# The last four modulation chunks of a hybrid mLSTM layer: row sums on VectorE, or partial sums on VectorE and a column reduction on TensorE

## The chip, the cores and the metric

The kernel runs on one core of a Trainium2 chip. The metric is the device time of one execution in microseconds (us). The median over three executions of the kernel before is 1634.9 us (1633.83 to 1635.89).

## The reference

One layer of a diffusion backbone is computed for 128 context tokens and 512 latent tokens (640 together, `NT`), with a model width of 1024. The part that matters here is the modulation. Two conditioning vectors (`c_ctx` for context, `c` for latent) pass through silu and a 1024 x 6144 matrix, and the 6144 results are cut into six chunks that scale and shift the activations:

```
mod_ctx = silu(c_ctx) @ w_mod[l] + b_mod[l]
mod_lat = silu(c) @ w_mod[l] + b_mod[l]
sh1, sc1, g1, sh2, sc2, g2 = jnp.split(mod, 6, axis=-1)
h = x * (1 + sc1) + sh1
out, finals = mixer(h, l, p, init, fourier_fn)
x = layer_norm(ALPHA * x + g1 * out, ...)
h2 = x * (1 + sc2) + sh2
a, u = jnp.split(h2 @ p['w_ffn_in'][l], 2, axis=-1)
f = (jax.nn.silu(a) * u) @ p['w_ffn_out'][l]
x = layer_norm(ALPHA * x + g2 * f, ...)
```

The mixer projects `h`, runs a bidirectional mLSTM over four heads and a Fourier branch, gates both, and multiplies by the output matrix.

## The kernel before

Activations are kept transposed: 128 channels on the partitions, 640 tokens along the free axis. Weights arrive in units of 128 x 1024 floats (512 KB). SyncE (SP) loads a unit into one of two slots of `raw`; GpSimd (POOL) splits it into `w_hi` and `w_lo` (L598, L602); TensorE multiplies it (`unit_cols`, L694, three products hi-hi, lo-hi, hi-lo for each block of 128) and then increments `units_done`. POOL may split unit u when unit u-2 has been multiplied, and SP may load unit u when unit u-2 has been split. Nothing plans the order: each engine runs the list of its block in the program, and SP's queue is strictly in that order, waits included.

The stages in time are: modulation chunks 0 and 1 and the first projection; Fourier branch; four heads of mLSTM (to about 834 us); the *gate units* (`U_GA`, 8 units, the rest of them to 898 us); the *mixing units* (`U_MIX`, 16 units, two for each output tile j = 0..7, to 1020 us); the output projection (`U_OUT`, 8 units); the first layer norm; the feed-forward input units (`U_FF1`, to 1445 us); the feed-forward output units (`U_FF2`) and the last layer norm.

During the gate units the normalised mLSTM output is read back. For each of four rounds i, SP loads two sets of four tiles `yg_st` (L523), a weight unit after each set (L525), and two modulation tiles after each (L528). ScalarE (ACT) runs the sigmoid of the gate (L1322) and rounds the four tiles to `yg_hi` (L1340). VectorE (DVE) makes the four `yg_lo` (L1729), which free the `yg_st` slots, and then handles two modulation tiles. So a later set of `yg_st`, and the weight unit queued behind it on SP, can only be issued as the `yg_lo` operations go.

In the mixing units, DVE has for each j three operations on the result (L1740, L1742, L1744) and then two or three modulation tiles (`MIX_MODS`); SP queues the loads of those tiles (L464) behind the weight loads of the same j (L538).

The modulation is done in two ways.

- Chunk 0 (8 tiles, in the first 44 us): `mod_add` multiplies a tile of 128 input channels x 1024 outputs by silu(c) as a per-partition scalar and adds it to `mod_sum`, once for each of the two conditioning vectors; after 8 tiles `mod_chunk` (L711) reduces over the partitions on TensorE, and `mod_finish` (L1422) adds the bias. (Chunk 1 is done by TensorE alone, L725.)
- Chunks 2 to 5 (32 tiles, the rest of the kernel): the matrix is stored transposed, a tile is 128 outputs x 1024 input channels. `mod_tile` (L1428) is a multiply with a row sum, once for each conditioning vector (64 operations, each followed by a read of the accumulator into `mod_sb`). The second operand, silu(c) repeated on all partitions (`silu_row`, 128 x 2048 floats), shares memory with `mod_sum`; SP loads it from `c_rows` (1 MB, L517) when the heads' stores have landed, ahead of the first `yg_st` loads, and ACT applies silu (L1333) ahead of the third gate unit's sigmoid.

```
for m in range(KD):
    for g in range(2):
        ins = mm(psum[:, bank, 2 * m + g:2 * m + g + 1],
                 mod_sum[:, g, m * P:(m + 1) * P], ones_r[:, 0:1].bitcast(F32),
                 start=True, stop=True)
```

Sixteen such matmuls make a `mod_chunk`; the 128 x 128 piece of `mod_sum` is the stationary operand, and one column of ones streams past.

Of the kernel before, what the change touches and what calls it, by code (L numbers as in the profile page):

```python
# [23 lines left out]
F32 = mybir.dt.float32  # L24
F32R = mybir.dt.float32r
I32 = mybir.dt.int32
ALU = mybir.AluOpType
ACT = mybir.ActivationFunctionType

P = 128  # L30
# [7 lines left out]
H = 4  # L38
# [3 lines left out]
KD = DMODEL // P  # L42
# [50 lines left out]
def build(nc, wunits, wmod1, wmod2, xT, cT, c_rows, bmod, consts, dft_c, dft_l, dft_x, wgate, gate_bias,  # L93
# [3 lines left out]
    with ctx:  # L97
# [36 lines left out]
        silu_row = mod_sum  # L134
# [115 lines left out]
        prod_m = at("prod_m", [P, UW], F32, cm)  # L250
# [15 lines left out]
        prod_l = at("prod_l", [P, UW], F32, [cf[0] + 4 * 2 * UW])  # L266
# [44 lines left out]
        c_row_in = sem("c_row_in")  # L311
        c_row_ok = sem("c_row_ok")
# [97 lines left out]
        def joined(pair):  # L410


            a = 2 * pair * 512 + 512 - CUT
            return flat[:, a:a + NT]
# [28 lines left out]
        def _(sp):  # L443
# [73 lines left out]
            sp.dma_start(silu_row[:], c_rows).then_inc(c_row_in, 16)  # L517
# [164 lines left out]
        def _(pe):  # L682
# [318 lines left out]
            for j in range(KD):  # L1001
                p = j % 2
                pe.wait_ge(taken[p], A_MIX + j // 2 + 1)
                for q in range(2):
                    pe.wait_ge(ygs_ok, 4 + 8 * q + 8)
                    unit_cols(joined(p), U_MIX + 2 * j + q, q, yg_hi, yg_lo, k0=8 * q, first=(q == 0), last=(q == 1))

# [28 lines left out]
            with pe.Fori(1, KF) as i:  # L1036
                for p in range(2):
                    pe.wait_ge(taken[p], A_FF1 + i + 1)
                    unit_cols(joined(p), U_FF1 + 2 * i + p, p, h2_hi, h2_lo)
            pe.wait_ge(f_ok, KF + 1)  # L1040
# [29 lines left out]
        def _(act):  # L1070
# [261 lines left out]
            act.wait_ge(c_row_in, 16)  # L1332
            A_(silu_row[:], silu_row[:], ACT.Silu).then_inc(c_row_ok, 1)  # L1333
# [57 lines left out]
        def _(v):  # L1391
# [36 lines left out]
            def mod_tile(t, ring, prod):  # L1428

                m = MOD1 + t  # L1430
                v.wait_ge(c_row_ok, 1)
                v.wait_ge(mod2_in[t % 2], 16 * (t // 2) + 16)
                for g, done in enumerate((mod_sum0, mod_sum1)):
                    v.wait_ge(mod_sum1 if g == 0 else mod_sum0, KD + t + g)
                    v.tensor_tensor_reduce(out=prod[:], in0=ring[:, t % 2, :], in1=silu_row[:, g, :], scale=1.0,  # L1435
                                           scalar=bmod_sb[:, m, g:g + 1], op0=ALU.mult, op1=ALU.add,
                                           accum_out=mod_sb[:, m, g:g + 1]).then_inc(done, 1)
# [288 lines left out]
            for i in range(H * KV // 4):  # L1726
                for r in range(4):
                    v.wait_ge(ygs_hi_ok, 4 * i + r + 1)
                    v.scalar_tensor_tensor(out=yg_lo[:, 4 * i + r, :], in0=yg_st[:, r, :],  # L1729
                                           scalar=gain_h[:, 4 * i + r:4 * i + r + 1],  # L1730
                                           in1=yg_hi[:, 4 * i + r, :].bitcast(F32),
                                           op0=ALU.mult, op1=ALU.subtract).then_inc(ygs_ok, 1)
                for m in range(2):
                    mod_tile(2 * i + m, mod_ring, prod_m)
            for j in range(KD):
# [9 lines left out]
                for m in range(MIX_MODS[j], MIX_MODS[j + 1]):  # L1745
                    mod_tile(KD + m, mod_ring, prod_m)
            v.wait_ge(mod_sum1, 4 * KD)
# [57 lines left out]
            for i in range(KD):  # L1805
                gated_unit(i)
                mod_tile(3 * KD + i, mod_late, prod_l)
            with v.Fori(KD, KF) as i:
                gated_unit(i)
            v.wait_ge(mod_sum1, 5 * KD)  # L1810
# [149 lines left out]
```

## Time and profile before

| | |
|---|---|
| median of three executions | 1634.9 us |
| the profiled execution, its time | 1633.83 us |
| its span in the profile | 1632.0 us |
| mean granted TensorE clock | 0.963 |
| TensorE / VectorE / ScalarE / GpSimd busy | 1497.3 / 674.7 / 319.8 / 798.2 us |
| modulation loads during the gate and mixing units | 24 of 512 KB |

The 1.8 us between the profiled execution's time and its span lie outside the span. Times in the rows are from the start of the span. PE is TensorE's matmuls and PEld its weight loads. SPq and ACTq are DMA issues; a merged DMA row in a timeline lasts from its first issue to its last one. In brackets stands the idle time in front of a row with what ended it.

### The profile page before, as it was taken

Reading aid. Unit: us, or ns where it says so; the run is one execution under the profiler, and the core shown is the slowest. Engines: PE = TensorE matmul, PEld = TensorE weight load, DVE = VectorE, ACT = ScalarE, POOL = GpSimd, SP = SyncE. Lnnn points to the kernel's source line nnn. Section 1 sums busy time; section 2 is a strip of 40 time slices with the busy share of each in tenths; the row PEclk is TensorE's granted clock in tenths of the full one; section 3 lists DMA queues with packets and bytes.
Section 4 is the critical chain, followed back from the end, with each engine's and each line's share of the span. In section 5 each row is a group of like instructions: output and inputs, shape, how many; then the busy total and the mean of one; then the engine's idle time right before and its main releaser. Section 6 shows DMA issues by size and latency. Waiting matters only on the chain.

```text
span 1632.0 us, 24364 instructions
## 1 busy us (share of the span) xinstructions
PE 1497.3 (92%) x9761; PEld 1455.1 (89%) x9761; DVE 674.7 (41%) x1088; ACT 319.8 (20%) x493; POOL 798.2 (49%) x365
## 2 busy tenths in 40 slices
PE   7999899999999899899887998794999999999994
PEld 7997799989889789899887998794999999999994
DVE  6412500227526624733659797457334111101114
ACT  0412211212112112122132000125121112200002
POOL 2541255552363253154235775355666666656662
PEclk9999999999999999899998999896999999999997
DMA  8210122311321321131146453311333221242221
GB/s 341 88 65 27 47 90 89 129 65 65 108 72 56 105 84 53 51 129 65 40 167 224 155 178 133 116 64 46 123 115 116 77 77 66 76 151 80 72 71 64
DMA packets 56236, 160.77 MB, mean 99 GB/s; under 512 B 5960, under 2 KB 20560, under 8 KB 54872
## 3 DMA queue, kind: packets, MB, share of 16 engines
q1 hardware_dynamic: 39608, 146.78, 24.9%
q10 hardware_dynamic: 16544, 12.82, 2.5%
q8 instruction: 59, 0.97, 0.2%
q14 instruction: 25, 0.20, 0.0%
HBM read 142.24 MB, written 17.33 MB: 98 GB/s over the span
## 4 chain that ended last, share of the span: by engine, by line
PE 72%; DVE 14%; issue 5%; ACT 3%; DMA 3%; POOL 2%; SPq 1%; ACTq 0%; DVEq 0%; POOLq 0%
PE psum L690 56%; PE psum L960 7%; PE psum L933 2%; PE psum L775 2%; DVE prod_m L1435 2%; PE psum L889 1%; DMA mod_first<-in_wmod 1%; DVE yg_lo L1729 1%; PE psum L750 1%; DMA raw<-in_wunits 1%; PE psum L1014 1%; POOL r_all L662 1%; DVE m_sb L1742 1%; DVE h_sb L1561 1%; PE psum L849 1%
## 5 line engine op out<-in xcount | busy, mean ns | idle before, releaser
L598 POOL TENSOR_TENSOR w_hi<-raw,zero 128x1024 fp32r<-128x1024 f32 x156 | 302.1, 1936 | 642.6 <-PE psum L690 536.7
L602 POOL TENSOR_TENSOR w_lo<-raw,w_hi 128x1024 fp32r<-128x1024 f32 x164 | 415.8, 2535 | 83.4 <-ACT w_hi L1120 71.2
L690 PE MATMUL psum<-h_hi,w_hi 128*128 128x256 f32 x1600 | 373.5, 315 | 48.5 <-POOL w_lo L602 21.0
L690 PE MATMUL psum<-h_lo,w_hi 128*128 128x256 f32 x1600 | 370.6, 313 | 0.0
L690 PE MATMUL psum<-h_hi,w_lo 128*128 128x256 f32 x1600 | 369.5, 312 | 0.0
L690 PEld LDWEIGHTS psum<-h_hi,w_hi 128*128 128x128 f32 x1600 | 295.7, 192 | 53.1 <-issue 28.4
L690 PEld LDWEIGHTS psum<-h_lo,w_hi 128*128 128x128 f32 x1600 | 297.9, 192 | 0.0
L690 PEld LDWEIGHTS psum<-h_hi,w_lo 128*128 128x128 f32 x1600 | 297.2, 192 | 0.0
L1435 DVE CUSTOM_DVE_ANT_0 prod_m<-mod_ring,mod_sum,bmod_sb 128x1024 f32<-128x1024 f32 x48 | 89.4, 1862 | 3.8 <-DVE mod_sb L1435 2.1
L1800 DVE TENSOR_TENSOR ff_sb<-psum,s_sb 128x640 f32<-128x640 f32 x22 | 18.1, 825 | 160.3 <-PE psum L690 148.7
L690 PE MATMUL psum<-f_hi,w_hi 128*128 128x256 f32 x352 | 81.3, 312 | 2.8 <-DVE f_lo L1401 2.8
L690 PE MATMUL psum<-f_lo,w_hi 128*128 128x256 f32 x352 | 80.8, 311 | 0.0
L690 PE MATMUL psum<-f_hi,w_lo 128*128 128x256 f32 x352 | 80.7, 310 | 0.0
L1760 DVE SCALAR_TENSOR_TENSOR r_t<-psum,mod_sb,x_all 128x128 f32<-128x128 f32 (+1 forms) x16 | 8.1, 547 | 145.7 <-PE psum L690 145.7
L933 PE MATMUL psum<-v_hi,p_hi 128*128 128x256 f32 (+1 forms) x176 | 52.2, 297 | 16.7 <-DVE h_sb L1561 16.7
L690 PEld LDWEIGHTS psum<-f_hi,w_hi 128*128 128x128 f32 x352 | 64.2, 190 | 3.1 <-DVE f_lo L1401 3.1
L690 PE MATMUL psum<-yg_hi,w_hi 128*128 128x256 f32 (+1 forms) x256 | 59.2, 313 | 7.2 <-POOL w_lo L602 7.2
L690 PEld LDWEIGHTS psum<-f_hi,w_lo 128*128 128x128 f32 x352 | 64.7, 190 | 0.0
L690 PEld LDWEIGHTS psum<-f_lo,w_hi 128*128 128x128 f32 x352 | 64.7, 190 | 0.0
L960 PE MATMUL psum<-w_lo,h_hi 128*128 128x512 f32 x160 | 62.3, 389 | 0.0
L960 PE MATMUL psum<-w_hi,h_lo 128*128 128x512 f32 x160 | 62.3, 389 | 0.0
L960 PE MATMUL psum<-w_hi,h_hi 128*128 128x512 f32 x160 | 62.2, 389 | 0.0
(274 smaller groups left out, 2501.3 us busy)
## 6 DMA issues: line engine op xcount, KB each, us to landing
raw<-in_wunits SPq DMA_DIRECT2D x164, 512.0 KB, 3.5
mod_ring<-in_wmod SPq DMA_DIRECT2D x24, 512.0 KB, 3.7
mod_first<-in_wmod SPq DMA_DIRECT2D x16, 512.0 KB, 11.8
yg_dram<-yg_sb ACTq DMA_DIRECT2D x20, 256.0 KB, 2.7
yg_st<-yg_dram SPq DMA_DIRECT2D x16, 320.0 KB, 3.7
c_raw<-in_stateC SPq DMA_DIRECT2D x4, 1028.0 KB, 5.8
mod_late<-in_wmod SPq DMA_DIRECT2D x8, 512.0 KB, 4.7
raw<-in_wunits SPq DMA_DIRECT2D x8, 384.0 KB, 2.9
```

Of the source, the lines that this page charges most:

```text
L598: pool.tensor_tensor(hi, src, zero[:, 0:1].broadcast_to([P, src.shape[1]]), ALU.add)\
L602: pool.tensor_tensor(lo, src, hi.bitcast(F32), ALU.subtract).then_inc(w_split, 1)
L662: pool.tensor_scalar(r_all[:, j, :], r_all[:, j, :], aln[:, 0, j:j + 1], aln[:, 1, j:j + 1], ALU.mult, ALU.add).then_inc(x1_ok, 1)
L690: ins = mm(out[:, a:z], w[:, slot, cols], x[:, k, a:z], start=(start and n == 0), stop=(stop and n == 2))
L750: ins = mm(psum[:, 4 + tt % 3, 0:XW], u[:, g % 2, k, tt * P:(tt + 1) * P], d[:, k, :], start=(n == 0), stop=(n == 5))
L775: ins = mm(out[0:m, span], x[:, t, cc], d, start=(t == tiles[0] and n == 0), stop=(t == tiles[-1] and n == len(jobs) - 1), skip_group_chec ...
L849: ins = mm(psum[:, bank, :], a, b[:, :, :].rearrange("p a b -> p (a b)"), start=(j == 0), stop=(j == len(jobs) - 1))
L889: ins = mm(s_tiles[:, s, :], a[:, d, wlat(s)], b[:, d, tq], start=(n == 0), stop=(n == 3 * KQ - 1))
L933: ins = mm(outs[d], a, b, start=(n == 0), stop=(n == len(jobs) - 1))
L960: ins = mm(psum[:, v_banks[tt], :], x[:, k, tt * P:(tt + 1) * P], w[:, q % 2, cols], start=(k == 0 and n == 0), stop=(k == KD - 1 and n == 2))
L1435: v.tensor_tensor_reduce(out=prod[:], in0=ring[:, t % 2, :], in1=silu_row[:, g, :], scale=1.0, scalar=bmod_sb[:, m, g:g + 1], op0=ALU.mult ...
L1800: v.tensor_tensor(ff_sb[:], joined(1), s_sb[:], ALU.mult).then_inc(taken[1], 1)
```

## The change

Chunks 2 to 5 are computed as chunk 0 is. The matrix for them is stored untransposed, so that each tile is 128 input channels x 1024 outputs (same size, same number of loads). `mod_tile` becomes a wait and a `mod_add`. Four more `mod_chunk` calls are put on TensorE: after mixing tile j = 0, after j = 4, after the last mixing tile, and after the last feed-forward input unit. The first tile of a chunk waits on VectorE until the reduction of the chunk before is done (`mod_done`). Four `mod_finish` read the results. The 1 MB load of `c_rows`, its silu, and the product buffers go.

```diff
@@ SyncE, after the heads' stores
-            sp.dma_start(silu_row[:], c_rows).then_inc(c_row_in, 16)
@@ TensorE, mixing units (inside the loop over j, after the two units of j)
+                if j == 0:
+                    pe.wait_ge(st_dve, 2 * H)
+                    pe.wait_ge(st_act, 3 * H)
+                    mod_chunk(1, 7)
+                elif j == 4:
+                    mod_chunk(2, 6)
+            mod_chunk(3, 5)
@@ TensorE, after the feed-forward input units
+            mod_chunk(4, 7)
             pe.wait_ge(f_ok, KF + 1)
@@ ScalarE, before the loop over gate units
-            act.wait_ge(c_row_in, 16)
-            A_(silu_row[:], silu_row[:], ACT.Silu).then_inc(c_row_ok, 1)
@@ VectorE
-            def mod_tile(t, ring, prod):
-
-                m = MOD1 + t
-                v.wait_ge(c_row_ok, 1)
+            def mod_tile(t, ring):
+
+                if t % KD == 0 and t:
+                    v.wait_ge(mod_done, 2 + t // KD)
                 v.wait_ge(mod2_in[t % 2], 16 * (t // 2) + 16)
-                for g, done in enumerate((mod_sum0, mod_sum1)):
-                    v.wait_ge(mod_sum1 if g == 0 else mod_sum0, KD + t + g)
-                    v.tensor_tensor_reduce(out=prod[:], in0=ring[:, t % 2, :], in1=silu_row[:, g, :], scale=1.0,
-                                           scalar=bmod_sb[:, m, g:g + 1], op0=ALU.mult, op1=ALU.add,
-                                           accum_out=mod_sb[:, m, g:g + 1]).then_inc(done, 1)
+                mod_add(KD + t, ring[:, t % 2, :], t % KD)
@@ VectorE, after the mixing units
-            v.wait_ge(mod_sum1, 4 * KD)
+            v.wait_ge(mod_done, 5)
+            for c, bank in ((2, 7), (3, 6), (4, 5)):
+                ins = mod_finish(c, bank)
+            own(ins)
@@ VectorE, after the feed-forward input units
-            v.wait_ge(mod_sum1, 5 * KD)
+            v.wait_ge(mod_done, 6)
+            own(mod_finish(5, 7))
@@ host
-        "wmod2": wm[:, 2 * UW:].T.reshape(4 * KD, P, UW),
+        "wmod2": wm[:, 2 * UW:].reshape(KD, P, 4, UW).transpose(2, 0, 1, 3).reshape(4 * KD, P, UW),
```

## Rows read from the trace of the kernel before

**Rows 1.** The page: busy time, share, instructions; and the chain by engine.

```profile
PE 1497.3 (92%) x9761; PEld 1455.1 (89%) x9761; DVE 674.7 (41%) x1088; ACT 319.8 (20%) x493; POOL 798.2 (49%) x365
PE 72%; DVE 14%; issue 5%; ACT 3%; DMA 3%; POOL 2%; SPq 1%; ACTq 0%; DVEq 0%; POOLq 0%
```

**Rows 2.** Instructions of single lines: duration ns min/median/max, first and last start.

```profile
L716 PEld LDWEIGHTS psum<-ones_r,mod_sum x32: 288/333/333, 37.2 to 43.8; 128*128 128x128 f32 x32
L725 PEld LDWEIGHTS psum<-c_silu,mod_first x128: 285/333/338, 6.5 to 37.0; 128*128 128x128 f32 x128
L1435 DVE CUSTOM_DVE_ANT_0 prod_m<-mod_ring,mod_sum,bmod_sb x48: 1271/1285/3412, 855.4 to 1013.8; 128x1024 f32<-128x1024 f32 x48
L1419 DVE SCALAR_TENSOR_TENSOR mod_sum<-mod_first,c_silu,mod_sum x14: 1272/1272/3361, 16.6 to 35.8; 128x1024 f32<-128x1024 f32 x14
L1417 DVE TENSOR_SCALAR mod_sum<-mod_first,c_silu x2: 741/1730/2719, 13.3 to 15.9; 128x1024 f32<-128x1024 f32 x2
```

**Rows 3.** Weight loads grouped by form, in 1004 to 1008 and in 1010 to 1014.

```profile
L690 PEld LDWEIGHTS psum<-yg_lo,w_hi 128*128 128x128 f32 x6 | 1.9, 330 | 0.0
...
L690 PEld LDWEIGHTS psum<-yg_lo,w_hi 128*128 128x128 f32 x9 | 1.6, 188 | 0.0
```

**Rows 4.** Windows: length, busy PE, PEld, DVE, ACT, POOL; granted clock, DMA share, GB/s.

```profile
37.00:44.00 7.00, 7.00 (x34) 7.00 (x34) 0.30 (x2) 0.00 (x0) 0.00 (x0) 1.00 0.02 6
...
890.76:897.80 7.04, 7.04 (x48) 7.04 (x49) 7.00 (x5) 0.00 (x0) 4.79 (x2) 1.00 0.44 148
...
897.80:911.90 14.10, 14.10 (x98) 14.10 (x98) 6.66 (x6) 0.71 (x1) 9.63 (x4) 1.00 0.50 189
...
1003.82:1008.70 4.88, 4.85 (x18) 4.88 (x19) 4.67 (x5) 0.00 (x0) 4.80 (x2) 0.50 0.04 7
1025.31:1029.20 3.89, 3.86 (x14) 3.89 (x15) 1.87 (x5) 0.00 (x0) 0.00 (x0) 0.50 0.97 411
```

**Rows 5.** Timeline of the weight loads: the ends of five idle stretches.

```profile
854.83 0.50 PEld L690 LDWEIGHTS psum<-h_hi,w_hi 128*128 128x128 f32 x2 [6.73 <-POOL w_lo L602]
...
890.76 0.30 PEld L690 LDWEIGHTS psum<-h_hi,w_hi 128*128 128x128 f32 x2 [2.99 <-POOL w_lo L602]
...
1003.82 0.50 PEld L690 LDWEIGHTS psum<-yg_hi,w_hi 128*128 128x128 f32 x2 [7.45 <-issue]
...
1025.31 0.50 PEld L690 LDWEIGHTS psum<-mg_hi,w_hi 128*128 128x128 f32 x2 [5.19 <-issue]
...
1447.66 0.30 PEld L690 LDWEIGHTS psum<-f_hi,w_hi 128*128 128x128 f32 x2 [3.11 <-DVE f_lo L1401]
```

**Rows 6.** Timeline of DVE in the gate units, and its seventh modulation tile's end.

```profile
848.45 7.01 DVE L1729 SCALAR_TENSOR_TENSOR yg_lo<-yg_st,gain_h,yg_hi 128x640 fp32r<-128x640 f32 x4 [13.44 <-ACT yg_hi L1340]
855.38 1.28 DVE L1435 CUSTOM_DVE_ANT_0 prod_m<-mod_ring,mod_sum,bmod_sb 128x1024 f32<-128x1024 f32 x1
...
860.71 7.00 DVE L1729 SCALAR_TENSOR_TENSOR yg_lo<-yg_st,gain_h,yg_hi 128x640 fp32r<-128x640 f32 x4
...
904.59 0.08 DVE L1435 DVE_READ_ACCUMULATOR2_ANT mod_sb<- 128x1 f32 x1
```

**Rows 7.** Timeline of ACT around the silu of the repeated row.

```profile
843.69 1.92 ACT L1333 ACTIVATE mod_sum<-mod_sum 128x2048 f32<-128x2048 f32 x1 [5.92 <-DMA mod_sum<-in_c_rows]
845.62 1.28 ACT L1322 ACT_TABLE_LOAD   x1
846.92 0.70 ACT L1322 ACTIVATE ga_sb<-psum 128x640 f32 x1
847.52 2.97 ACT L1340 ACTIVATE yg_hi<-yg_st,gain_h 128x640 f32 x4
```

**Rows 8.** Timeline of SP's queue in the gate and mixing units.

```profile
838.97 0.33 SPq L517 DMA_DIRECT2D mod_sum<-in_c_rows  x1
...
842.03 0.33 SPq L525 DMA_DIRECT2D raw<-in_wunits  x1
...
880.64 0.33 SPq L525 DMA_DIRECT2D raw<-in_wunits  x1
...
976.62 14.41 SPq L464 DMA_DIRECT2D mod_ring<-in_wmod  x3
```

**Rows 9.** Timeline of POOL at the end of the mixing units.

```profile
1020.47 1.89 POOL L598 TENSOR_TENSOR w_hi<-raw,zero 128x1024 fp32r<-128x1024 f32 x1 [1.16 <-PE psum L690]
```

More of the change, by code:

```diff
@@ L90, with build @@
 MAGIC = float(0x5F3759DF)
-def build(nc, wunits, wmod1, wmod2, xT, cT, c_rows, bmod, consts, dft_c, dft_l, dft_x, wgate, gate_bias,
+def build(nc, wunits, wmod1, wmod2, xT, cT, bmod, consts, dft_c, dft_l, dft_x, wgate, gate_bias,
           stateC, m0_rows, m0_bcast, gainT, lnT, ln_rows,
@@ L133, in build @@
         mod_sum = at("mod_sum", [P, 2, UW], F32, em_at)
-        silu_row = mod_sum
         assert em_at[0] <= top[0]
@@ L249, in build @@
         mod_ring = at("mod_ring", [P, 2, UW], F32, cm)
-        prod_m = at("prod_m", [P, UW], F32, cm)
         cg = [ring_end]
@@ L265, in build @@
         mod_late = at("mod_late", [P, 2, UW], F32, [cf[0]])
-        prod_l = at("prod_l", [P, UW], F32, [cf[0] + 4 * 2 * UW])
         ln_row = at("ln_row", [P, 2, DMODEL], F32, cf)
@@ L310, in build @@
         mod_sum1 = sem("mod_sum1")
-        c_row_in = sem("c_row_in")
-        c_row_ok = sem("c_row_ok")
         mod_done = sem("mod_done")
@@ L1733, in _ @@
                 for m in range(2):
-                    mod_tile(2 * i + m, mod_ring, prod_m)
+                    mod_tile(2 * i + m, mod_ring)
             for j in range(KD):
@@ L1745, in _ @@
                 for m in range(MIX_MODS[j], MIX_MODS[j + 1]):
-                    mod_tile(KD + m, mod_ring, prod_m)
-            v.wait_ge(mod_sum1, 4 * KD)
+                    mod_tile(KD + m, mod_ring)
+            v.wait_ge(mod_done, 5)
+            for c, bank in ((2, 7), (3, 6), (4, 5)):
+                ins = mod_finish(c, bank)
+            own(ins)
             lg = ln_sb[:, 0, :].unsqueeze(2).broadcast_to([P, KD, 2])
@@ L1806, in _ @@
                 gated_unit(i)
-                mod_tile(3 * KD + i, mod_late, prod_l)
+                mod_tile(3 * KD + i, mod_late)
             with v.Fori(KD, KF) as i:
                 gated_unit(i)
-            v.wait_ge(mod_sum1, 5 * KD)
+            v.wait_ge(mod_done, 6)
+            own(mod_finish(5, 7))
             def row_stats(j):
@@ L1937 @@
         "wunits": wunits, "wmod1": np.concatenate([wm[:, 0:UW].reshape(KD, P, UW), blocks(wm[:, UW:2 * UW])]),
-        "wmod2": wm[:, 2 * UW:].T.reshape(4 * KD, P, UW),
+        "wmod2": wm[:, 2 * UW:].reshape(KD, P, 4, UW).transpose(2, 0, 1, 3).reshape(4 * KD, P, UW),
         "xT": x.reshape(NT, KD, P).transpose(2, 1, 0), "cT": cc.reshape(2, KD, P).transpose(2, 1, 0),
-        "c_rows": np.repeat(cc[None], P, axis=0),
         "bmod": np.repeat(a["b_mod"][0].reshape(NMOD, P).T[:, :, None], 2, axis=2),
```

## Prediction

> **What bounds the kernel now.** I began with the busy times and the chain on the page [rows 1]: TensorE is busy 1497.3 us of 1632.0 and carries 72% of the chain, VectorE carries 14% though it is busy for only 41%. So work added to TensorE lengthens the kernel unless it falls into one of its idle stretches, and VectorE matters in places only. The second step was to find those places. The timeline of the weight loads [rows 5] gives TensorE's idle stretches around the modulation work: 6.73 us ending at 854.83, 2.99 ending at 890.76, 7.45 ending at 1003.82, 5.19 ending at 1025.31, 3.11 ending at 1447.66. Between them TensorE is continuous: 14.10 us busy in 14.10 for a mixing tile [rows 4].
>
> The third step was what ends them. In the gate units it is POOL's split, POOL waits for a weight load, and SP can issue that load only when VectorE has freed the four `yg_st` slots in front of it. VectorE runs without a gap there: four `yg_lo` from 848.45, modulation from 855.38, the next four from 860.71 [rows 6], a round of 12.26 us for one weight unit that TensorE multiplies in 7.04 [rows 4]. So from 848.45 to the last gate unit (load issued at 880.64 [rows 8], multiplied from 890.76) the stage goes at VectorE's pace, and its start is set by what comes ahead of the first `yg_lo`.
>
> **What is removed at the start of that stage.** SP issues the 1 MB load at 838.97 [rows 8]; ACT waits 5.92 us for it, spends 1.92 on silu and 1.28 on a table load, and only at 846.92 reaches the sigmoid and at 847.52 the first `yg_hi` [rows 7]. Without the load and the silu, ACT is free when the third gate unit ends, 7.04 us before the fourth's end at 848.1 (854.83 - 6.73), so at 841.0. A table load (1.28) and the sigmoid (0.70) remain: first `yg_hi` at about 843.0, first `yg_lo` 0.9 later (847.52 to 848.45 before), at 843.9. The `yg_st` loads are issued 0.67 earlier and with 1 MB less in front, and should have landed by then. That is 848.45 - 843.9 = 4.55 us. Bounds: nothing below 3 (if the loads, not ACT, are last), 5.9 above (ACT's whole wait). SP's weight load of 842.03 sheds the same traffic, so POOL isn't left behind.
>
> **VectorE's operations.** Before: 1285 ns median, and four of them take 860.71 - 855.38 = 5.33 us with their accumulator reads. After: `mod_add` is 1272 ns median, 741 at best for the first tile of a chunk [rows 2]. Both kinds stretch to the same 3.4 us at worst beside POOL (3412 and 3361), so contention gives nothing either way. I take 1.2 us from start to start without the accumulator read: 4.8 for a round, 3.75 for the first. Two rounds of modulation lie ahead of the load at 880.64: (5.33 - 3.75) + (5.33 - 4.8) = 2.1 us. **Gate units together: -4.55 - 2.1 = -6.6 us**, with bounds -4 and -8. In the mixing units VectorE is off the path, and the same saving is worth nothing there except below.
>
> **What `mod_chunk` costs on TensorE.** Its 32 weight loads start from 37.2 to 43.8 [rows 2], 0.213 us apart, 6.86 us in all. But this was at the lower clock: a load lasts 333 ns there, as the 330 ns of loads at granted 0.50 and not the 188 ns at 1.00 [rows 3]. (The window 37 to 44 shows 1.00 [rows 4]; the loads' own length says otherwise, and I go by it.) In the mixing units the clock is full. If the spacing follows the clock, a chunk is 6.86 / 2 = 3.43 us; the upper bound is 6.86. I take 3.43, since the load's length does scale.
>
> The Trainium skill, *TensorE: Matmul & The Clock Gate*, section "LDWEIGHTS (loading the stationary operand)", gives a load as its columns over 1.2, in ns, which is 107 for 128 columns, 3.4 us by that page for the 32; the trace's spacing at the lower level is twice that, so the page would be right only at the full clock.
>
> Then the clock itself. From 6.5 to 44 us TensorE did little else than such matmuls with one or two columns, 128 + 32 of them, and the loads stayed at 333 ns throughout: they don't raise the clock. So a chunk should count as idleness. Idle stretches of 7.45 and 5.19 us were followed by 4.88 and 3.89 us of work at 0.50 [rows 4, 5], a loss of half, 2.4 and 1.9 us; the one of 2.99 ending at 890.76 was followed by 7.04 us at 1.00. A chunk lies between. I take a loss of 2.1 us, and 0.25 for draining and refilling around it; bounds 0 and 3.4 (a low stretch twice that of the rows, half of it filled by the chunk itself).
>
> **The four chunks, each in its place.**
> - After j = 0 (about 905 us): its sums are complete (VectorE's tile 7 ended at 904.67 even without the 6.6 us [rows 6]), so it starts at once; TensorE was continuous here [rows 4]. Fully exposed: 3.43 + 2.1 + 0.25 = 5.8.
> - After j = 4: same, 5.8. It isn't repaid by the 7.45 us stretch ahead of j = 7. That one comes from SP: its third modulation load for j = 5 waits for a tile which VectorE handles only after j = 5's units, so its queue is held from 976.62 to 991.03 [rows 8] with the next weight load behind. All of this is tied to the end of j = 5 and moves with it.
> - After the last mixing unit: TensorE stands idle 5.19 us while POOL splits the second output unit (from 1020.47 [rows 9]), which waits for `units_done`, and that is incremented ahead of the chunk. 3.43, even with a clock that falls on the way, fits in. Cost 0; if a chunk is 6.86, 1.7.
> - After the feed-forward input units: 3.11 us idle, waiting for `f_lo`. 3.43 + 0.25 - 3.11 = 0.6. If a chunk is 6.86, 4.0.
>
> VectorE's new waits (`mod_done` for tiles 8, 16, 24) cost nothing: behind each wait stand modulation tiles only, and VectorE reaches it 5.4 us after TensorE's units ended (three operations), later than a chunk's end. VectorE no longer runs 0.4 us late behind each tile in the mixing units, so the stall at j = 7 shrinks by about 0.5. The `mod_finish` are 16 columns wide, under TensorE's output units.
>
> **Sum:** -6.6 + 5.8 + 5.8 + 0 + 0.6 - 0.5 = **+5.1 us**. On the profiled execution, 1633.83 + 5.1 = **1638.9 us**, which is 4.0 or 0.24% above the median 1634.9. A measurement of this kernel tells about 0.2% (3.3 us) from no change, so the forecast is "slower", narrowly.
>
> **The rivals.**
> 1. *The clock stays up through the chunks*, and both exposed ones cost 3.43 + 0.25: -6.6 + 7.4 + 0.6 - 0.5 = +0.9, 1634.7 us, no change. For it: TensorE counts as busy through a chunk (7.00 of 7.00 [rows 4]), and an idle stretch of 2.99 didn't lower the clock. Against it: 37 us of the same matmuls never raised it. Decides if the chunk's 3.4 us aren't taken for idleness. The Trainium skill, *TensorE: Matmul & The Clock Gate*, section "Part 1: The HAM clock gate", says that low clock is the default and that activity releases it; whether one column past a full weight load is activity it doesn't say. Chance 0.22. At the edge of the gate units' bound (-8) it would be 1633.3.
> 2. *A chunk takes 6.86 us whatever the clock*: -6.6 + 2 x (6.86 + 2.35) + 1.7 + 4.0 - 0.5 = +17.0, 1650.8 us. For it: that is the only duration on record. Against it: rows 3. Chance 0.12.
> 3. *The gate units give nothing back*, since the DMA engines or the `yg_st` loads hold them as VectorE did: +5.1 + 4.55 = +9.7 (the 2.1 us of VectorE's own operations stay), 1643.5 us. Against it: ACT's 5.92 us wait is plainly for the removed load. Chance 0.08.
> 4. *Faster*: in the gate units POOL's splits now fall beside the modulation tiles instead of beside `yg_lo`, and the four `yg_lo` take less than 7.0 us. If each of the two counted rounds shed another 3 us, the sum is 5.1 - 6 = -0.9; with the clock staying up, -5: 1628.8. Against it: the operations stretch alike on either side. Chance 0.08.
>
> The forecast has the remaining 0.50; its own range is 1636 to 1642. The 8-in-10 range is 1632.5 to 1646. Slower by over 0.2%: most of the forecast (0.36), rivals 2 and 3, 0.56 together. Within 0.2%: the rest of the forecast and most of rival 1, 0.33. Faster: 0.11.
>
> **What would show it.** In the profile after: no ACT wait at 837 to 843 and the first `yg_lo` near 844; the last gate unit from about 884; a round of VectorE near 11.8 us. The loads of L716 in the mixing units 0.107 us apart and 188 ns long (0.213 and 333 would be rival 2 or an early fall of the clock), a chunk 3.4 to 5 us, and behind it a window at 0.50 for some 4 us. The idle stretch ahead of the output units filled, at no cost. The forecast is wrong by more than its range if the chunk's pace doesn't follow the clock, or if `mod_chunk` waits for VectorE's sums.

## The result, and the profile after

The changed kernel takes 1644.8 us (median of 8 runs, 1639.7 to 1650.8) where the kernel before took 1634.4 on the same chip (8 runs, 1632.3 to 1637.6). The ratio is 1.006 with a 95% interval of 1.0041 to 1.0081, so it is slower by about 9.8 us. The profiled execution took 1646.2 us, its span is 1644.4, which is 12.4 above the span before (1632.0). The forecast was slower by 5.1.

The page first: busy time, share and instructions by engine, then the chain by engine, to be read against [rows 1]. TensorE has 21.1 us and 128 matmuls more. The matmuls are the four chunks, 32 each; the chunks' own lengths, in the timeline below, add up to 16.8 us, and most of the rest is the slower clock behind them. The chain's share of VectorE fell from 14% to 12%.

```profile
PE 1518.4 (92%) x9889; PEld 1476.9 (90%) x9889; DVE 652.5 (40%) x1028; ACT 314.3 (19%) x489; POOL 801.4 (49%) x365
...
PE 75%; DVE 12%; issue 4%; ACT 3%; DMA 2%; POOL 2%; SPq 1%; ACTq 0%; DVEq 0%; POOLq 0%
```

**TensorE's side.** The timeline of the weight loads, with the four chunks (L710) and the ends of the idle stretches in brackets, as in [rows 5]:

```profile
851.29 0.50 PEld L684 LDWEIGHTS psum<-h_hi,w_hi 128*128 128x128 f32 x2 [4.42 <-POOL w_lo L596]
...
882.15 0.50 PEld L684 LDWEIGHTS psum<-h_hi,w_hi 128*128 128x128 f32 x2 [14.20 <-POOL w_lo L596]
...
912.76 4.96 PEld L710 LDWEIGHTS psum<-ones_r,mod_sum 128*128 128x128 f32 x32
...
976.26 3.65 PEld L710 LDWEIGHTS psum<-ones_r,mod_sum 128*128 128x128 f32 x32 [0.40 <-DVE mod_sum L1419]
...
1015.08 0.50 PEld L684 LDWEIGHTS psum<-yg_hi,w_hi 128*128 128x128 f32 x2 [5.53 <-issue]
...
1031.69 4.47 PEld L710 LDWEIGHTS psum<-ones_r,mod_sum 128*128 128x128 f32 x32
...
1036.96 0.50 PEld L684 LDWEIGHTS psum<-mg_hi,w_hi 128*128 128x128 f32 x2 [0.80 <-issue]
...
1456.55 3.71 PEld L710 LDWEIGHTS psum<-ones_r,mod_sum 128*128 128x128 f32 x32
```

A chunk at full clock takes 3.65 us, and the others are longer where the clock falls inside them. The single loads of L710 (the unchanged chunk 0 of the first 44 us among them) run from 186 to 338 ns with a median of 192. The windows show the clock: length, busy PE, granted clock, DMA share, GB/s. Behind the chunks at 912.76, 976.26 and 1456.55 it is 0.51, 0.58 and 0.60 for some 4 us, although TensorE counts as busy throughout.

```profile
912.80:917.60 4.80, 4.80 (x35) 0.73 0.12 45
918.00:922.00 4.00, 4.00 (x17) 0.51 0.61 171
976.30:979.90 3.60, 3.60 (x33) 1.00 0.70 226
980.00:984.00 4.00, 4.00 (x18) 0.58 0.72 263
...
1456.60:1460.20 3.60, 3.60 (x34) 1.00 0.65 160
1460.50:1464.00 3.50, 3.50 (x17) 0.60 0.54 167
```

The unexpected row above is the idle stretch of 14.20 us ending at 882.15: it lies in the gate units, which were to become shorter.

**The gate units.** ACT first, to be read against [rows 7]. The wait of 5.92 us and the silu are gone, and with the silu both table loads around it: the forecast had kept one of 1.28 us. The sigmoid stands at 840.25 instead of 846.92.

```profile
840.25 0.71 ACT L1324 ACTIVATE ga_sb<-psum 128x640 f32 x1 [7.23 <-PE psum L684]
841.27 1.78 ACT L1340 ACTIVATE yg_hi<-yg_st,gain_h 128x640 f32 x2 [0.32 <-DMA yg_st<-yg_dram]
```

VectorE, against [rows 6]. Its first `yg_lo` is at 842.21 instead of 848.45. From 848.23 to 877.07 it runs without a gap, from 861.06 on also at its full speed, 3.26 us for four `yg_lo` where the kernel before needed 7.0 beside POOL.

```profile
842.21 1.75 DVE L1725 SCALAR_TENSOR_TENSOR yg_lo<-yg_st,gain_h,yg_hi 128x640 fp32r<-128x640 f32 x2 [8.43 <-ACT yg_hi L1340]
...
848.23 3.56 DVE L1417 TENSOR_SCALAR mod_sum<-mod_ring,c_silu 128x1024 f32<-128x1024 f32 x2 [1.49 <-DMA mod_ring<-in_wmod]
851.71 2.47 DVE L1419 SCALAR_TENSOR_TENSOR mod_sum<-mod_ring,c_silu,mod_sum 128x1024 f32<-128x1024 f32 x2
854.10 7.03 DVE L1725 SCALAR_TENSOR_TENSOR yg_lo<-yg_st,gain_h,yg_hi 128x640 fp32r<-128x640 f32 x4
861.06 4.86 DVE L1419 SCALAR_TENSOR_TENSOR mod_sum<-mod_ring,c_silu,mod_sum 128x1024 f32<-128x1024 f32 x4
865.84 3.26 DVE L1725 SCALAR_TENSOR_TENSOR yg_lo<-yg_st,gain_h,yg_hi 128x640 fp32r<-128x640 f32 x4
869.02 4.86 DVE L1419 SCALAR_TENSOR_TENSOR mod_sum<-mod_ring,c_silu,mod_sum 128x1024 f32<-128x1024 f32 x4
873.81 3.26 DVE L1725 SCALAR_TENSOR_TENSOR yg_lo<-yg_st,gain_h,yg_hi 128x640 fp32r<-128x640 f32 x4
877.22 12.11 DVE L1419 SCALAR_TENSOR_TENSOR mod_sum<-mod_ring,c_silu,mod_sum 128x1024 f32<-128x1024 f32 x4 [0.15 <-DMA mod_ring<-in_wmod]
```

POOL's timeline of the same stretch, and L592 over the whole kernel (ns min/median/max, first and last start). Against a median of 1892 ns, one split took 11440. It began at 867.38, 8.52 us after POOL's last operation and while VectorE was in its run, and ended at 878.82, 1.75 us after VectorE's first pause, the 0.15 us before 877.22. TensorE's 14.20 us were the wait for the `w_lo` behind it, the second half of the same unit's split.

```profile
856.01 2.85 POOL L596 TENSOR_TENSOR w_lo<-raw,w_hi 128x1024 fp32r<-128x1024 f32 x1
867.38 11.44 POOL L592 TENSOR_TENSOR w_hi<-raw,zero 128x1024 fp32r<-128x1024 f32 x1 [8.52 <-DMA raw<-in_wunits]
878.89 3.20 POOL L596 TENSOR_TENSOR w_lo<-raw,w_hi 128x1024 fp32r<-128x1024 f32 x1
...
L592 POOL TENSOR_TENSOR w_hi<-raw,zero x156: 1466/1892/11440, 10.5 to 1608.0; 128x1024 fp32r<-128x1024 f32 x148, 128x768 fp32r<-128x768 f32 x8
```

I take as the length of the gate units the time between two sigmoids of ACT on `ga_sb`, of the second gate unit and of the last: 830.64 to 898.11 before, 67.5 us; 829.41 to 899.05 after, 69.6 us. The 12.4 us of the span divide so: entry -1.2, gate units +2.1, from there to the output units' start +10.7 (127.2 to 137.9), from there to the end +0.7 (606.7 to 607.4). Over the layer's nine profiles (before, after and the seven below), the entry (start to the second gate unit's sigmoid), which no edit touches, takes from 829.0 to 837.0 us, and the last part 605.1 to 607.4. So a total of one run carries several us that are not the edit's, and the stages are compared by their own lengths.

### The profile page after: what moved, and what is told of

The parts are those of the page before. It is cut to its first block, busy times and chain, and to the rows that moved or that the text cites. A ratio compares the mean times of both kernels' runs of the same rounds, so it can differ in the third digit from the quotient of the medians.

```text
span 1644.4 us, 24556 instructions
## 1 busy us (share of the span) xinstructions
PE 1518.4 (92%) x9889; PEld 1476.9 (90%) x9889; DVE 652.5 (40%) x1028; ACT 314.3 (19%) x489; POOL 801.4 (49%) x365
## 4 chain that ended last, share of the span: by engine, by line
PE 75%; DVE 12%; issue 4%; ACT 3%; DMA 2%; POOL 2%; SPq 1%; ACTq 0%; DVEq 0%; POOLq 0%
PE psum L684 58%; PE psum L954 7%; PE psum L927 2%; PE psum L769 2%; PE psum L710 1%; PE psum L883 1%; DVE mod_sum L1419 1%; DMA mod_first<-in_wmod 1%; POOL w_hi L592 1%; PE psum L744 1%; PE psum L1015 1%; DMA raw<-in_wunits 1%; POOL r_all L656 1%; DVE h_sb L1557 1%; PE psum L843 1%
## 5 line engine op out<-in xcount | busy, mean ns | idle before, releaser
L592 POOL TENSOR_TENSOR w_hi<-raw,zero 128x1024 fp32r<-128x1024 f32 x156 | 307.1, 1969 | 652.2 <-PE psum L684 560.1
L1419 DVE SCALAR_TENSOR_TENSOR mod_sum<-mod_ring,c_silu,mod_sum 128x1024 f32<-128x1024 f32 x42 | 73.6, 1806 | 2.4 <-DMA mod_ring<-in_wmod 2.4
```

What stands on the lines that cost most here:

```text
L592: pool.tensor_tensor(hi, src, zero[:, 0:1].broadcast_to([P, src.shape[1]]), ALU.add)\
L1419: v.scalar_tensor_tensor(out=a, in0=w, scalar=s_, in1=a, op0=ALU.mult, op1=ALU.add)\
```

## The experiments

Twelve further runs follow, one of them the changed kernel again. `pause`, `rows_back` and `pause_rows` are compared with a median of 1636.5 us of the kernel before (12 runs, 1631.4 to 1644.6), `chunks_only`, `late_rows` and `pause_spread` with 1634.1 (23 runs). The length of a stage comes from one profile of each kernel.

**1. `port`: POOL and VectorE alone.** A program without the layer's computation: three additions like POOL's split, by themselves or beside runs of 4, 8 or 12 `mod_add` of VectorE.

> Not the layer: a small program that leaves the whole computation out and writes placeholders. In ten cases GpSimd runs three additions of 128x1024 (each alone about 1.9 us) beside a burst of VectorE operations of 128x1024 (alone 1.27 us): 0, 4, 8, 12 multiply-adds with two SBUF tensors issued back to back and started ahead of GpSimd; 4, 8, 12 of them where each waits for the one before; 8 operations with one SBUF tensor; and 8 multiply-adds, unpaced and paced, started when GpSimd is already in its run. Theory A (VectorE operations that follow each other without a break keep GpSimd's operation out until the burst ends): the first GpSimd operation lasts about 5, 10 and 15 us for bursts of 4, 8 and 12, about 2 to 3 us in the paced cases, and with GpSimd ahead it is VectorE that is stretched to 2.5 to 3.3 us an operation. Theory B (the two share evenly, and the 11.4 us operation in the changed kernel had another cause such as DMA traffic): no GpSimd operation over 4 us in any case, and burst length doesn't matter.

Timeline of POOL (three additions, first alone, then beside VectorE):

```profile
9.96 5.59 POOL L77 TENSOR_TENSOR pdst<-psrc,zero 128x1024 f32<-128x1024 f32 x3 [9.13 <-DVEq L91]
15.83 8.58 POOL L77 TENSOR_TENSOR pdst<-psrc,zero 128x1024 f32<-128x1024 f32 x3 [0.28 <-DVEq L106]
```

8.58 us, and the same for runs of 4, 8 and 12, also where each VectorE operation waits for the one before it. (Beside operations with one SBUF tensor the three take 6.98, and 6.57 where POOL starts first.) The engines slow each other down (POOL 1.89 to 2.87 an operation), but POOL is not kept out. That a run without pauses by itself keeps POOL out is refuted, for arrivals at its beginning.

**2. `pause`: the changed kernel, each modulation operation waiting for the one before it.** In `mod_add`, for the modulation tiles of chunks 2 to 5 (I call this paced):

```
-                    if n:
+                    if paced:
+                        v.wait_ge(mod_sum1 if g == 0 else mod_sum0, n + g)
+                    elif n:
                         v.wait_ge(done, n)
```

> The changed kernel, but each modulation operation of chunks 2 to 5 waits for the one just before it (as the row sums of the kernel before did), which costs VectorE about 0.1 us each. Theory A (GpSimd is kept out by VectorE operations without a break): no GpSimd operation over 4 us in the gate units, the last gate unit starts 5 to 7 us before the kernel before's 890.8, and the time falls from 1644.8 by 6 to 9 us to 1636 to 1639, with less spread. Theory B (the gate units are held by DMA traffic or by the loads of yg_st, not by the port): the extra waits bring nothing, 1643 to 1647.

1641.9 us, ratio 1.0038 (1.0018 to 1.0058), span 1637.2. It is +5.4 us by the medians and +6.2 by the ratio, above the 1636 to 1639 that I had expected. The change had a ratio of 1.006 (1.0041 to 1.0081); the two intervals overlap, so the times alone don't separate the two kernels. Timelines of VectorE and of POOL:

```profile
861.54 5.30 DVE L1421 SCALAR_TENSOR_TENSOR mod_sum<-mod_ring,c_silu,mod_sum 128x1024 f32<-128x1024 f32 x4
866.75 6.98 DVE L1727 SCALAR_TENSOR_TENSOR yg_lo<-yg_st,gain_h,yg_hi 128x640 fp32r<-128x640 f32 x4
```

```profile
867.83 2.35 POOL L592 TENSOR_TENSOR w_hi<-raw,zero 128x1024 fp32r<-128x1024 f32 x1 [8.49 <-DMA raw<-in_wunits]
870.25 2.80 POOL L596 TENSOR_TENSOR w_lo<-raw,w_hi 128x1024 fp32r<-128x1024 f32 x1
```

The same split in the same place takes 2.35 us, after 8.49 us in which POOL stood idle (8.52 with the change). No POOL operation in the gate units is longer than 2.87. The stage takes 61.8 us, 5.7 less than before, where 6.6 were forecast. The pauses cost VectorE 0.44 us per four operations, 0.11 each. A second profile of a paced kernel, `pause_spread` below, has a stage of 62.2 us, and its arrival after 8.46 us is served in 2.38.

**3. `rows_back` and `pause_rows`: the 1 MB load and its silu put back,** ahead of the first `yg_st` and `yg_hi`, into the changed kernel and into `pause`. They serve nothing there but the wait.

```
+            sp.dma_start(mod_sum[:], c_rows).then_inc(c_row_in, 16)
...
+            act.wait_ge(c_row_in, 16)
+            A_(mod_sum[:], mod_sum[:], ACT.Silu).then_inc(c_row_ok, 1)
...
+                if t == 0:
+                    v.wait_ge(c_row_ok, 1)
```

> The changed kernel with one part undone: the 1 MB load and its silu are put back at their places (result unused), so the gate units begin as late as in the kernel before; the modulation operations stay unpaced. If the removed load gave its 4.5 us and only GpSimd's being kept out ate it, this is slower than the changed kernel by up to 4.5 us, unless the other phase of the operations spares GpSimd: 1640 to 1650. If the removed load was worth nothing, the same as the changed kernel within 1 us and with the same long GpSimd operation.

> The paced kernel with the 1 MB load and its silu put back. Against the paced kernel it prices the removed load alone. My theory: 4.5 us slower than the paced one (bounds 3 and 5.9), 1641 to 1643, and the first yg_lo back near 848. Rival (the load was hidden anyway, or the DMA engines would hold the stage instead): within 1 us of the paced one.

`rows_back`: 1646.3 us, ratio 1.0067 (1.0047 to 1.0087). `pause_rows`: 1645.8 us, 1.0057 (1.0037 to 1.0076). The intervals of the four kernels overlap, and these two medians differ by 0.5 us, so the times show no gain of the pacing here. I go by the stage's own length, one profile each: 73.7 us for `rows_back`, 66.3 for `pause_rows`, against 69.6 and 61.8 without the load. The load and the silu cost 4.5 us in the paced pair and 4.1 in the other (forecast 4.55); the 4.1 holds two kept-out splits of different length and proves little. The pacing saves 7.4 and 7.8 of the stage. That `pause_rows` isn't faster in the total is in its profile an entry of 837.0 us, where `rows_back` has 830.8; for the other runs it stays open. Once VectorE's run has begun, no split of `pause_rows` arrives later than 7.12 us after POOL's last operation, so it is the weaker test of the two. In `rows_back` too a split is kept out; VectorE's last row here runs to 890.95, and POOL's ends at 892.70, again 1.75 later:

```profile
882.90 3.26 DVE L1732 SCALAR_TENSOR_TENSOR yg_lo<-yg_st,gain_h,yg_hi 128x640 fp32r<-128x640 f32 x4
886.09 4.86 DVE L1424 SCALAR_TENSOR_TENSOR mod_sum<-mod_ring,c_silu,mod_sum 128x1024 f32<-128x1024 f32 x4
```

```profile
884.24 8.46 POOL L595 TENSOR_TENSOR w_hi<-raw,zero 128x1024 fp32r<-128x1024 f32 x1 [8.32 <-DMA raw<-in_wunits]
```

**4. `port2`: 24 phases of arrival.** Without the layer's computation: VectorE runs 16 operations without a pause (four `yg_lo`, four `mod_add`, twice), and POOL's split arrives 0.04 us later each time, up to 1.4 us into the run.

> Not the layer: the whole computation is left out and placeholders are written. 24 cases. In each, VectorE issues sixteen operations without a break as the gate units do (four of 128x640 with the form of yg_lo, four modulation multiply-adds of 128x1024, and both again, some 16 us alone), and one GpSimd addition of 128x1024 (alone 1.9 us) arrives after a ScalarE copy whose length grows by 48 columns from case to case, so at another moment of the first VectorE operations. In the first small program, where GpSimd arrived at the start of a burst, the two shared evenly (2.9 us each), which refutes the simple form of theory A. Theory A2: it depends on the moment of arrival; in some cases the GpSimd operation is kept out until VectorE stops, and lasts over 8 us and ends about 1.8 us after the burst; in the others it takes 2 to 3 us. Theory B: the port always shares, no GpSimd operation over 4 us in any of the 24 cases, and the 11.4 us operation needs another cause that this program doesn't have (DMA traffic, TensorE, the compute program's own waits).

Two neighbouring cases of POOL's timeline:

```profile
207.97 1.89 POOL L89 TENSOR_TENSOR pdst<-psrc,zero 128x1024 fp32r<-128x1024 f32 x1 [16.01 <-ACT a_dst L76]
225.91 2.59 POOL L89 TENSOR_TENSOR pdst<-psrc,zero 128x1024 fp32r<-128x1024 f32 x1 [16.05 <-ACT a_dst L76]
```

The split's length falls from 2.23 to 1.89 as it arrives nearer to the end of VectorE's operation, jumps to 2.59 when the next has begun, and falls again. So it waits for the end of the current VectorE operation and then has its turn, and VectorE's four `yg_lo` take 4.91 us instead of 3.26. For these 24 cases this is what the Trainium skill, *SBUF — State Buffer*, section "SBUF: two separate sides", says: where a VectorE operation with two SBUF inputs meets a GpSimd operation that reads SBUF, whichever starts first has the shared ports for its whole instruction, and the other is blocked. The phase within one operation explains nothing longer.

**5. `chunks_only`: the kernel before with the four chunks on TensorE,** in the change's places; the modulation stays on VectorE's reductions, so the chunks' sums are not used.

```
+                if j == 0:
+                    pe.wait_ge(st_dve, 2 * H)
+                    pe.wait_ge(st_act, 3 * H)
+                    mod_chunk(1, 7)
+                elif j == 4:
+                    mod_chunk(2, 6)
+            mod_chunk(3, 5)
...
+            mod_chunk(4, 7)
```

> The kernel before with the four column reductions added on TensorE at the places of the change (over whatever lies in mod_sum, results unused); VectorE, ScalarE and SyncE as before. It prices TensorE's part alone. From the changed kernel's trace: 6.7 us after j = 0, 5.8 after j = 4, nothing after the last mixing unit, 0.7 after the feed-forward input units, less 1 to 2 at the stall of j = 7: +11 to +13 us, ratio 1.007 to 1.008. A rival that puts the loss elsewhere (the gate units alone) expects +4 to +6.

1645.4 us, ratio 1.0067 (1.0051 to 1.0082), span 1643.6: +11.4 us. Gate units 66.6 us, where the kernel before has 67.5; nothing differs there, so a length of this stage repeats to about 1 us. From there to the output units' start it is 138.6 instead of 127.2, +11.4. The sum of the forecast's TensorE terms, 5.8 + 5.8 + 0.6 - 0.5, is 11.7.

**6. `late_rows`: the kernel before, the 1 MB load behind the first four `yg_st`** and the silu behind the first four `yg_hi`.

```
-            sp.dma_start(silu_row[:], c_rows).then_inc(c_row_in, 16)
...
+                    if i == 0 and q == 0:
+                        sp.dma_start(silu_row[:], c_rows).then_inc(c_row_in, 16)
...
```

> The kernel before with the 1 MB load moved behind the first four yg_st loads, and its silu behind the first four yg_hi on ScalarE; the row sums stay (the two loops over gate units are written out). If that load's place is worth what the removal gave (4.5 us between the two paced kernels' traces), this is 3 to 4.5 us faster than the kernel before, ratio 0.997 to 0.998, and the first yg_lo comes near 844. Rival: the modulation tiles then wait for the silu, or GpSimd meets another phase, and nothing is gained (within 1.5 us).

1633.5 us, ratio 0.9988 (0.9976 to 1.0), 12 runs: 2 us faster by the ratio, with an interval that touches no difference, and less than the 3 to 4.5 us expected. VectorE's timeline shows what took the rest:

```profile
856.79 1.71 DVE L1437 CUSTOM_DVE_ANT_0 prod_m<-mod_ring,mod_sum,bmod_sb 128x1024 f32<-128x1024 f32 x1 [4.53 <-DMA mod_ring<-in_wmod]
```

The load moved behind `yg_st` stands in front of the modulation tiles, and VectorE waits there. The stage takes 66.3 us. That is 1.2 less than before, but `chunks_only`, with an unchanged stage, has 66.6, so no gain in the stage is shown.

**7. `pause_spread`: `pause`, with the two exposed chunks spread** over the next mixing unit, two of their one-column matmuls after each of its eight blocks.

```
+                    if between is not None and b < nb - 1:
+                        between(b)
```

> The paced kernel, with the reductions after j = 0 and j = 4 spread over the next unit (two of their matmuls after each of its eight blocks) instead of in one piece. If the fall of TensorE's clock behind a piece of one-column matmuls costs what the trace shows (a low stretch after each), this saves 2 to 3 us for each of the two: 4 to 6 us faster than the paced kernel, which was 1641.9 beside 1636.5 of the kernel before, so a ratio of 1.000 to 1.002 and no window at 0.50 behind j = 0 and j = 4. Rival: the breaks between blocks cost as much, or the clock falls anyway: within 1.5 us of the paced kernel, ratio near 1.004.

1637.4 us, ratio 1.002 (1.0011 to 1.0028), 12 runs, span 1633.6. From the gate units' end to the output units' start it takes 135.4 us, where `pause` takes 139.0: 3.6 less, where 4 to 6 were expected. Windows over the two stretches in which the chunks now lie, and over what follows the first chunk in `pause`:

```profile
920.00:935.00 15.00, 15.00 (x104) 1.00 0.52 179
980.00:990.00 10.00, 10.00 (x70) 1.00 0.31 105
```

```profile
908.98:913.00 4.02, 4.02 (x16) 0.50 0.38 130
```

Spread, the chunks leave the clock at its upper level. This is the best version of the changed idea, and it doesn't beat the kernel before.

**8. `port3` and `port4`: later arrivals; transfers and a second POOL operation.** Again without the layer's computation: 36 arrivals from 1.2 to 4.0 us into a run of 24 operations; `port4` adds transfers all the time and a `w_lo` behind each `w_hi`.

> A program without the layer's computation: 36 times, VectorE runs 24 operations without a pause (four yg_lo of 640 columns, four mod_add of 1024, three times over) and POOL's w_hi operation arrives from 1.2 to 4.0 us after the first yg_lo has started, 0.08 us later each time. The long POOL operations of the layer arrived 1.34 and 1.54 us into such a run, where the program with 24 phases ended. Theory C (phase): from some phase on within the second yg_lo, about 1.3 us, POOL is kept out and its operation lasts until VectorE pauses, 20 us or more. Theory D (the phase isn't it; something else of the layer is): all 36 last 1.89 to 3 us.

> The same 36 phases, again without the layer's computation, but with transfers of 0.5 MB into SBUF running all the time, and with a second POOL operation (w_lo, two inputs) behind each first. Theory C: as in the program without transfers. Theory D1 (transfers, or POOL's own next operation, make the long one): some POOL operations here last 8 us or more, none without the transfers. Theory D2 (neither): all w_hi 1.89 to 3 us and all w_lo 2.3 to 3.3 us, and what makes the layer's long operation stays open.

In both all 36 `w_hi` last 1.89 to 2.98 us, and each `w_lo` 2.80 or 3.20. Transfers, a second operation and the phase are out. The small programs still had one thing in common: VectorE had run for at most 4 us when POOL came.

**9. `after_again`: the changed kernel, a second profile.**

> The changed kernel once more, for a second profile. If a POOL operation kept out in the gate units is what its time holds beyond the forecast's sum, this profile has one over 5 us there too (0.6), or its gate units take 61 to 63 us from the first to the last sigmoid and the span is near 1637 to 1640 (0.3). Rival: neither a long operation nor a short stage, 66 us or more without it, and the stage's loss has another cause (0.1).

1640.9 us (one run, beside 1638.2 for the kernel before), span 1639.1. Again one split is kept out, for 6.44 us:

```profile
858.28 2.87 POOL L596 TENSOR_TENSOR w_lo<-raw,w_hi 128x1024 fp32r<-128x1024 f32 x1
869.09 6.44 POOL L592 TENSOR_TENSOR w_hi<-raw,zero 128x1024 fp32r<-128x1024 f32 x1 [7.94 <-DMA raw<-in_wunits]
```

The stage takes 64.1 us here. So 61.8, 64.1 and 69.6 us go with a longest `w_hi` of 2.87 (paced), 6.44 and 11.44.

**10. `port5`: arrivals from 2 to 21 us.** Without the layer's computation, with transfers: VectorE runs 40 operations without a pause (40 us), and POOL's pair arrives about 1.08 us later in each second case. In the cases between, an additional pair of POOL runs beside the first operations.

> Once more without the layer's computation: VectorE runs 40 operations without a pause (about 40 us), transfers run beside it, and POOL's pair (w_hi, w_lo) arrives some 2 to 20 us after the start of that run; in half of the cases another pair of POOL has run beside its first operations, as in the layer. In the three traces with a long POOL operation VectorE had by then run without a pause for some 8 us or more with POOL idle; in the earlier small programs for at most 4. Theory E (how long VectorE has run unbroken decides): the arrivals after some 6 to 8 us are kept out until VectorE pauses, 20 to 30 us, the early ones last 1.89 to 3 us. Theory D2 (something that only the layer has): every w_hi lasts 1.89 to 3 us and every w_lo 2.8 to 3.3 us, and the cause stays open.

POOL's timeline: two neighbouring cases without the additional pair (VectorE's runs start at 376.91 and 468.34), then two with it. The number in brackets is how long POOL stood idle before.

```profile
383.56 1.96 POOL L106 TENSOR_TENSOR pdst<-psrc,zero 128x1024 fp32r<-128x1024 f32 x1 [43.39 <-ACT a_dst L88]
...
476.08 33.93 POOL L106 TENSOR_TENSOR pdst<-psrc,zero 128x1024 fp32r<-128x1024 f32 x1 [43.28 <-ACT a_dst L88]
...
984.15 1.96 POOL L106 TENSOR_TENSOR pdst<-psrc,zero 128x1024 fp32r<-128x1024 f32 x1 [7.65 <-ACT a_dst L88]
...
1076.93 31.15 POOL L106 TENSOR_TENSOR pdst<-psrc,zero 128x1024 fp32r<-128x1024 f32 x1 [8.73 <-ACT a_dst L88]
```

VectorE's timeline, the first and the last row of the run over which the second of them was kept out:

```profile
468.34 3.27 DVE L130 SCALAR_TENSOR_TENSOR y_lo<-src,scal,y_hi 128x640 fp32r<-128x640 f32 x4 [0.20 <-issue]
...
503.39 4.87 DVE L141 SCALAR_TENSOR_TENSOR acc<-src,scal,acc 128x1024 f32<-128x1024 f32 x4
```

An arrival 6.65 us into the run (383.56 - 376.91) is served at once. One 7.74 us into it (476.08 - 468.34) is kept out to the run's end: VectorE finishes at 508.26 and the split at 510.01, 1.75 later, the same distance as in the layer. With the additional pair the border lies between 7.65 and 8.73 us after POOL's last operation. It holds without exception: 16 arrivals before the border last 1.89 to 3.05 us, all 20 behind it 20.88 to 33.93. So the theory of the unbroken run is confirmed, with POOL's last turn as the start of the count where it has had one. The three long splits of the layer agree with it: they arrived 8.52, 8.32 and 7.94 us after POOL's last operation, into an unbroken run, which is inside the gap between 7.65 and 8.73 where `port5` has no case. In `pause` the arrival after 8.49 us is shared, since VectorE had paused, and so is one after 8.63 us in the kernel before.

## Why the prediction was right in sign and too small

- **The step that failed: "Gate units together: -4.55 - 2.1 = -6.6 us".** It measured +2.1 in the first profile and -3.4 in the second. Its two terms were not wrong in themselves: with VectorE paced, the stage gives back 5.7 us. What failed is the sentence under them, "so contention gives nothing either way", and with it "the operations stretch alike on either side" in rival 4. I read the stretched operations of [rows 2] as a port that two engines share at any time. The measured time lies in the wide range (1632.5 to 1646) and above the forecast's own (1636 to 1642); the direction rests on TensorE's terms, which held (below). `port2` shows turns of one instruction each, and `port5` shows that the turns end once VectorE has run for some 7 to 8 us without a pause and without a turn of POOL.
- **Why the change met it and the kernel before didn't.** Before, each of VectorE's reductions waited for the one before it and was followed by an accumulator read; four operations took 5.33 us with all that lay between them. The change removed precisely these. About half of the 2.1 us that the forecast booked as a gain (4.8 instead of 5.33 for a round, twice; the rest is the shorter first tile) are the pauses that let POOL in. That the waits do it is shown by `pause`, which differs from the change in them alone: all three profiles of kernels without them (`after`, `after_again`, `rows_back`) have a kept-out split, none of the three with them (`pause`, `pause_rows`, `pause_spread`) has one, and none of the three with the reductions (the kernel before, `chunks_only`, `late_rows`).
- **Does it account for the time?** The forecast's sum is +5.1, and `pause`, the change without this effect, is +6.2 us by its ratio (2.9 to 9.5). The change is +9.8 (6.7 to 13.2). The remaining 3.6 lie between what the second profile's kept-out split costs the stage (64.1 - 61.8 = 2.3) and the first's (7.8), so the effect is large enough. But the two intervals overlap, and only two runs of the changed kernel were profiled: how much of its median is the kept-out split isn't measured. The 11 us between its fastest and slowest run don't tell either: the 12 runs of the kernel before beside `pause` lie 13 apart.
- **ACT and the start of the stage: right in size, partly by luck.** The load and the silu are worth 4.5 us by `pause` against `pause_rows`, where 4.55 were summed. The make-up was another. No table load remained, so the first `yg_lo` stands at 842.21 where 843.9 was expected; with the entry 1.2 shorter, that is 5.0 us earlier in the stage. Then the `yg_st` loads were last for the third and fourth tile (VectorE idle 0.69 and 0.32), and VectorE waited 1.49 for its first modulation tile.
- **A chunk's length and pace: right.** 3.65 us where 3.43 + 0.25 were taken, loads of 192 ns, 0.11 us apart. Rival 2 (6.86 us) is out. The Trainium skill, *TensorE: Matmul & The Clock Gate*, section "LDWEIGHTS (loading the stationary operand)", gives 107 ns for a load; at the full clock the spacing is near it, though a single load lasts 192 ns, and at the lower level the spacing was 0.213 us.
- **The clock behind a chunk: right.** The output of mixing tile 1 stands 20.8 us behind that of tile 0, before 14.2: +6.6 where 5.8 was summed; here the clock fell within the chunk, so that it took 4.96. Behind j = 4 it is 19.6 instead of 14.1, +5.5; there the chunk waited 0.40 us for VectorE's sums, which the forecast had complete. VectorE's rows at the outputs of tiles 0 and 1, before and after, stand below this list. Rival 1 (the clock stays up) is out, and `pause_spread` shows the size of the clock's part by removing it: 3.6 us for the two.
- **The hidden chunks: right.** The one before the output units filled 5.19 us of idleness and left 0.80. The one behind the feed-forward input units cost 0.7 by the rest of the span (forecast 0.6), but that part varies by more from profile to profile, so the term isn't tested. The stall at j = 7 shrank from 7.45 to 5.53, by 1.9, where 0.5 was forecast. My reason for it (VectorE no longer late) was wrong: in the mixing units four modulation operations take 8.64 us beside POOL (row at 939.41 of the profile after), where a round took 8.71 before (917.66 to 926.37), so VectorE is still late behind a tile, and the stall is 5.68 in `chunks_only` and 5.48 in `late_rows`, where VectorE's operations are those of before, but 6.76 in `pause`. From the gate units' end to the output units' start the terms give 5.8 + 5.8 + 0 - 0.5 = 11.1, and it is 10.7.
- **Rival 3** (the gate units give nothing back, 1643.5) has nearly the right time by another mechanism: neither the DMA engines nor `yg_st` hold the stage, since paced it gives back 5.7 us. **Rival 4** looked at the right place, POOL against VectorE, and had its sign reversed: the four `yg_lo` did fall to 3.26 us, and that was the sign that POOL was standing.

The rows for the clock behind the first chunk (VectorE's first operation on the output of mixing tiles 0 and 1; the kernel before, then the changed one):

```profile
912.18 0.82 DVE L1740 TENSOR_TENSOR m_sb<-psum,ga_sb 128x640 f32<-128x640 f32 x1 [7.52 <-PE psum L690]
...
926.37 0.81 DVE L1740 TENSOR_TENSOR m_sb<-psum,ga_sb 128x640 f32<-128x640 f32 x1
```

```profile
913.13 0.82 DVE L1736 TENSOR_TENSOR m_sb<-psum,ga_sb 128x640 f32<-128x640 f32 x1 [23.80 <-PE psum L684]
...
933.92 0.82 DVE L1736 TENSOR_TENSOR m_sb<-psum,ga_sb 128x640 f32<-128x640 f32 x1 [11.56 <-PE psum L684]
```

What stays open: how much of the changed kernel's median the kept-out split makes; whether the border is one of time or of a number of instructions (in `port5`, without the additional pair, it falls between VectorE's seventh and eighth operation); which property of the operations it needs; and why in `after_again` VectorE gave way after two modulation operations, where its timeline shows no idle time of its own.

## What to carry to other kernels

An engine whose operations suddenly take their best time beside another that shares its ports has not gained anything: look for the other one's longest single operation (the maximum, not the mean; 11440 ns beside a median of 1892). When an edit removes small waits and reads between VectorE's operations, ask what used the gaps, and keep a dependent wait between them where POOL is on the critical path; here one ahead of each operation cost 0.44 us per round and the stage was 2.3 to 7.8 us shorter (fewer waits weren't tried). A block of one-column matmuls costs twice on TensorE, itself and the slow clock behind it (3.65 + 2 us), and spread between full-width blocks it costs little more than itself (`pause_spread`: 135.4 - 127.2 = 8.2 us for two).

## What the runs showed of the hardware that was not expected

- POOL and VectorE take turns by whole instructions at first: a split of 1.89 us takes 1.89 to 2.98, and VectorE's four `yg_lo` 3.26, 4.91 or 6.99 us beside none, one or two of POOL's operations.
- After 6.65 to 7.74 us of an unbroken run of VectorE, or 7.65 to 8.73 us after POOL's last operation within it, POOL gets no turn until VectorE pauses (`port5`; VectorE's operations have two SBUF inputs there); it was kept out for up to 33.93 us. A pause of 0.15 us was enough to let it in, and in `pause` pauses of 0.11 us kept it from being shut out.
- A kept-out operation ends 1.75 us after the run's end in the traces of the changed kernel, of `rows_back` and of `port5` (all 20 there, within 0.01 us).
- TensorE counts as busy all through a chunk, and the granted clock falls in it or right behind it all the same, to a mean of 0.50 to 0.60 over some 4 us.
